# Two attention mixers' norms applied behind the projections, and a home of their own for the forget gates' weights

## What is computed

```python
    h = x
    for i in range(DEPTH):
        j = i // 2
        h = h + FFN_RES_SCALE * swiglu_2(rms_norm(h, ffa_norm[i]), ffa_w_gate_up[i], ffa_w_down[i])
        hn = rms_norm(h, mix_norm[i])
        if i % 2 == 0:
            h = h + even_mixer(hn, ev_w_in[j], ev_sinks[j], ev_cq_norm[j], ev_w_uq[j],
                               ev_ckv_norm[j], ev_w_ukv[j], ev_w_out[j])
        else:
            h = h + odd_mixer(hn, od_w_in[j], od_b_f[j], od_w_out[j])
        h = h + FFN_RES_SCALE * swiglu_2(rms_norm(h, ffb_norm[i]), ffb_w_gate_up[i], ffb_w_down[i])
        gate = jax.nn.sigmoid(rms_norm(h, ple_norm[i]) @ ple_w_gate[i])
        h = h + gate * (p[i] @ ple_w_proj[i])
    return rms_norm(h, final_norm)
```

## Time and profile before

| | |
|---|---|
| runs, median (lowest to highest) | 4158.46 us (4157.44 to 4158.93), 3 runs |
| profiled execution | 4156.04 us |
| its span | 4154.2 us |
| PE busy | 3963.3 us, 95% |
| DVE, ACT, POOL busy | 2038.6, 1314.0, 457.4 us |
| mean granted clock of TensorE | 0.974 |

### The profile page before, as it was taken

One profiled execution on the slowest core, in us unless ns is written; L12 is line 12 of the kernel. 1 busy time (PEld: TensorE's weight loads), 2 busy tenths in 40 slices (PEclk: granted clock), 3 DMA queues, 4 the chain that ended last, 5 costly groups with the idle time before them and its releaser, 6 DMA issues.

```text
span 4154.2 us, 47658 instructions
## 1 busy us (share of the span) xinstructions
PE 3963.3 (95%) x19618; PEld 3262.3 (79%) x19618; DVE 2038.6 (49%) x3065; ACT 1314.0 (32%) x1964; POOL 457.4 (11%) x509
## 2 busy tenths in 40 slices
PE   8988889999989999999999989999999999999997
PEld 5678889788867887888888766888778878778886
DVE  6545565646356765433443444433543343553445
ACT  3225344322232223222322345322332232342223
POOL 0015543100001111000200034000100000010001
PEclk9899999999999999999999999999999999999999
DMA  6220002445231112332322311232232223012322
GB/s 208 77 71 1 1 1 92 129 150 188 83 108 50 45 42 92 99 104 90 103 92 90 103 59 41 90 104 77 96 108 91 90 83 103 21 52 91 105 79 75
DMA packets 344098, 351.26 MB, mean 85 GB/s; under 512 B 9547, under 2 KB 340107, under 8 KB 343628
## 3 DMA queue, kind: packets, MB, share of 16 engines
q1 hardware_dynamic: 343884, 348.22, 26.2%
HBM read 345.83 MB, written 2.10 MB: 84 GB/s over the span
## 4 chain that ended last, share of the span: by engine, by line
PE 89%; DVE 5%; ACT 3%; issue 2%; DMA 1%; POOL 0%; POOLq 0%; SPq 0%; DVEq 0%; ACTq 0%
PE ps L371 23%; PE ps L372 23%; PE ps L373 23%; PE ps L1495 4%; PE ps L2417 3%; PE ps L2374 1%; PE ps L378 1%; ACT whi L347 1%; PE ps L3292 1%; PE ps L458 1%; PE ps L460 1%; PE ps L459 1%; DVE wlo L353 1%; PE ps L3279 1%; PE ps L764 1%
## 5 line engine op out<-in xcount | busy, mean ns | idle before, releaser
L353 DVE TENSOR_TENSOR wlo<-raw,whi 128x2048 fp32r<-128x2048 f32 (+6 forms) x315 | 627.7, 1993 | 988.7 <-ACT whi L347 988.7
L371 PE MATMUL ps<-Xh,whi 128*128 128x512 f32 x2640 | 1042.4, 395 | 23.8 <-DVE wlo L353 10.0
L372 PE MATMUL ps<-Xl,whi 128*128 128x512 f32 x2640 | 1034.6, 392 | 0.0
L373 PE MATMUL ps<-Xh,wlo 128*128 128x512 f32 x2640 | 1034.2, 392 | 0.0
L347 ACT ACTIVATE whi<-raw 128x2048 fp32r<-128x2048 f32 (+6 forms) x315 | 521.8, 1656 | 1127.2 <-PE ps L373 1114.2
L371 PEld LDWEIGHTS ps<-Xh,whi 128*128 128x128 f32 x2640 | 499.5, 189 | 137.0 <-issue 31.2
L372 PEld LDWEIGHTS ps<-Xl,whi 128*128 128x128 f32 x2640 | 499.5, 189 | 105.9 <-issue 2.0
L373 PEld LDWEIGHTS ps<-Xh,wlo 128*128 128x128 f32 x2640 | 499.0, 189 | 106.4 <-issue 0.5
L371 PE MATMUL ps<-HDh,whi 128*128 128x512 f32 x1056 | 411.7, 390 | 0.0
L373 PE MATMUL ps<-HDh,wlo 128*128 128x512 f32 x1056 | 410.9, 389 | 0.0
L372 PE MATMUL ps<-HDl,whi 128*128 128x512 f32 x1056 | 410.8, 389 | 0.0
(11 more groups left out here) (556 smaller groups left out, 5592.4 us busy)
## 6 DMA issues: line engine op xcount, KB each, us to landing
raw<-in_ffn_w SPq DMA_DIRECT2D x44, 1024.0 KB, 5.3
raw<-in_ffa_w_gate_up SPq DMA_DIRECT2D x44, 1024.0 KB, 5.0
raw<-in_ffb_w_gate_up SPq DMA_DIRECT2D x44, 1024.0 KB, 5.0
mslot<-in_mod_w SPq DMA_DIRECT2D x28, 1024.0 KB, 7.9
raw<-in_mod_w SPq DMA_DIRECT2D x20, 1024.0 KB, 6.0
raw<-in_ab_w_in SPq DMA_DIRECT2D x14, 1024.0 KB, 5.2
raw<-in_ffn_w SPq DMA_DIRECT2D x16, 768.0 KB, 4.4
raw<-in_hy_w_in SPq DMA_DIRECT2D x12, 1024.0 KB, 5.1
```

What stands on the lines that cost most here:

```text
L353: dve.tensor_tensor(k.part(k.wlo, c), k.raw(c), k.part(k.whi, c).bitcast(F32), ALU.subtract).then_inc(*k.ev.put("dve_wlo", ("lo", n), ("ra ...
L371: pe.matmul(o, wh, xh, start=first, stop=False)
L372: pe.matmul(o, wh, xl, start=False, stop=False)
L373: return pe.matmul(o, wl, xh, start=False, stop=last)
```

## The change

n6 and n10 become LATE. Their sum of squares keeps the compact form: one group of sum matmuls stands behind the first run of the mixer (`late_sum_pe`), the spread one block later (`spread_pe`), and ACT copies the spread 1/rms to SBUF (`late_rs_act`). Every projection's eviction then multiplies by it, by column for transposed results (rstd) and as ACT's scale for av and fv (rcol). For fq and fk, DVE multiplies in the PSUM bank itself ("scaled"), and ACT and DVE read the bank as before. krope's multiply is on POOL. In the even mixer the sums for cq and ckv move from behind krx to behind aq's second block. The forget gates' chunk is loaded and split during a1's down part 1 into a buffer of its own; fq's second chunk takes the slot that this frees. negc and c2 move two blocks back.

```diff
+        "n6": ("mix", 0), "n10": ("mix", 1)}
+EARLY = ("n1", "n2", "n3", "n13")
+COMPACT = EARLY + ("n6", "n10")
@@ weights_in_order
+                if (st, part, cc) == ("a1", 1, 2):
+                    W.add(("fl", 0), "od_w_in_2", (0,), 0, 8, 3072, 16, False)
-            W.add(("fq", 0), "od_w_in_2", (0,), 0, 8, 0, 256)
-            lin("fl", "od_w_in_2", 8, 3072, 16)
-            for cc in range(1, 12):
+            for cc in range(12):
@@ new
+def late_sum_pe(k, pe, tag):
+    ps = k.psum[NB]
+    pe.wait_ge(*k.ev.at(("sqsum", tag, 7)))
+    for t in range(4):
+        ins = pe.matmul(ps[:, t:t + 1], k.sq[2][:, t * 128:t * 128 + 128], k.onesD[:, 0:1], start=t == 0, stop=t == 3)
+    ins.then_inc(*k.ev.put("pe_sum", ("summed", tag, 7)))
+def late_rs_act(k, act, tag):
+    act.wait_ge(*k.ev.at(("rstd", tag)))
+    act.activation(k.rstd[:, :], k.bk.of(("rs", tag))[:, :], ACT.Copy).then_inc(
+        *k.ev.put("act_std", ("rs copy", tag), ("out", "rs", tag)))
@@ even_pe
     lin_pe(k, pe, "cq", keys_of("cq", 256), 8, k.X, lambda kk: [("x", "n6", kk)], together=2)
+    late_sum_pe(k, pe, "n6")
     lin_pe(k, pe, "ckv", keys_of("ckv", 128), 8, k.X, none)
+    spread_pe(k, pe, "n6")
     lin_pe(k, pe, "krx", keys_of("krx", 128), 8, k.X, none)
--    pe.wait_ge(*ev.at("o256"))
...
-    lin_pe(k, pe, "aq", keys_of("aq", 512), 8, k.X, none)
+    def after(m, ends):
+        if m == 1:
+            pe.wait_ge(*ev.at("o256"))
...
+    lin_pe(k, pe, "aq", keys_of("aq", 512), 8, k.X, none, after=after)
@@ even_dve
+    h_norm_dve(k, dve, "n6")
     next_lo(k, dve, ("ckv", 0))
+    dve.wait_ge(*ev.at(("rs copy", "n6")))
+    for st, m, dst in (("cq", 0, k.cq[:, 0, :]), ("cq", 1, k.cq[:, 1, :]), ("ckv", 0, k.ckv[:, 0, :])):
+        dve.wait_ge(*ev.at(("mm", st, m, 0)))
+        dve.tensor_tensor(dst, k.bk.of((st, m, 0))[:, :], k.rstd[:, :], ALU.mult).then_inc(
+            *ev.put("dve_even", ("out", st, m, 0)))
@@ odd_pe
     def after(m, ends):
+        if m == 1:
+            late_sum_pe(k, pe, "n10")
         if m == 2:
+            spread_pe(k, pe, "n10")
+        if m == 4:
              ps = room(k, pe, ("negc",))
             pe.wait_ge(*ev.at("lf"))
...
-        if m == 5:
+        if m == 7:
             turned_pe(k, pe, "c2", k.cd, ALL7)
@@ odd_act
+    root_table(k, act)
     next_hi(k, act, ("fq", 0))
+    h_norm_act(k, act, "n10")
+    late_rs_act(k, act, "n10")
 ...
-            if m % 2:
-                next_hi(k, act, (st, (m // 2) * 256) if (st, m) != ("fq", 1) else ("fl", 0))
-            act.wait_ge(*ev.at(("mm", st, m, 0)))
+            if m % 2 and (st, m) != ("fq", 1):
+                next_hi(k, act, (st, (m // 2) * 256))
+            act.wait_ge(*ev.at(("scaled", st, m)))
@@ odd_dve
+    h_norm_dve(k, dve, "n10")
+    dve.wait_ge(*ev.at(("rs copy", "n10")))
+    dve.tensor_tensor(r[:, 0, :], k.bk.of(("fl", 0, 0))[0:16, :], k.rstd[0:16, :], ALU.mult).then_inc(
 ...
+            dve.wait_ge(*ev.at(("mm", st, m, 0)))
+            ps = k.bk.of((st, m, 0))[:, :]
+            dve.tensor_tensor(ps, ps, k.rstd[:, :], ALU.mult).then_inc(*ev.put("dve_odd", ("scaled", st, m)))
+            if m % 2 and (st, m) != ("fq", 1):
+                next_lo(k, dve, (st, (m // 2) * 256))
             dve.wait_ge(*ev.at(("hi", st, m)))
```

More of the change, by code:

```diff
@@ L408, in lin_together_pe @@
             if kk == kt - 1:
-                ins.then_inc(*k.ev.put("pe_lin", ("mm", st, m, 0), *([("used", c.n)] if ends else [])))
+                ins.then_inc(*k.ev.put("pe_lin", ("mm", st, m, 0), *([("used", c.n)] if ends and c.n is not None else [])))
 def lin_pe(k, pe, st, keys, kt, X, xkeys, widths=((0, 512),), among=ALL7, after=None, together=0, lead=(), first=0):
@@ L2942, in even_act @@
     ev = k.ev
-    act.wait_ge(*ev.at(("mm", "cq", 0, 0)))
-    act.activation(k.cq[:, 0, :], k.bk.of(("cq", 0, 0))[:, :], ACT.Copy).then_inc(*ev.put("act_even", ("out", "cq", 0, 0)))
-    square_act(k, act, "cq", 0, k.cq[:, 0, :], made=("out", "cq", 0, 0))
+    root_table(k, act)
     next_hi(k, act, ("cq", 0))
[L2947 to L2950, removed]
+    h_norm_act(k, act, "n6")
     next_hi(k, act, ("ckv", 0))
+    late_rs_act(k, act, "n6")
+    for i in range(2):
+        square_act(k, act, "cq", i, k.cq[:, i, :], made=("out", "cq", i, 0))
+    act.wait_ge(*ev.at(("out", "ckv", 0, 0)))
+    act.activation(k.rq[1][:, :], k.ckv[:, 0, :], ACT.Square).then_inc(*ev.put("act_sq", ("sq", "ckv", 0)))
     next_hi(k, act, ("krx", 0))
@@ L3039, in even_dve @@
     dve.wait_ge(*ev.now())
-    dve.tensor_tensor(kr, kr, kt, ALU.add).then_inc(*ev.put("dve_mla", "krope"))
-    rstd_dve(k, dve, "cq", k.rq[0][:, :])
-    rstd_dve(k, dve, "ckv", k.rq[1][:, :])
-    apply_dve(k, dve, "cq", lambda i: k.cq[:, i, :], 2, L, k.rq[0][:, :], lambda i: k.col("cq", i), None, k.CQ)
+    dve.tensor_tensor(kr, kr, kt, ALU.add).then_inc(*ev.put("dve_mla", "krope sum"))
     for m in range(4):
@@ L3110, in even_pool @@
     pool.memset(k.kz[0:64, 1, 1, :], 0.0).then_inc(*ev.put("pool_mla", "kz zero"))
+    pool.wait_ge(*ev.at("krope sum"))
+    pool.tensor_tensor(k.krr[64:128, :], k.krr[64:128, :], k.rstd[64:128, :], ALU.mult).then_inc(
+        *ev.put("pool_mla", "krope"))
     pool.wait_ge(*ev.at(("mm", "av", 0, 3)))
@@ L3145, in odd_mem @@
     k.c2 = k.sb("c2", [128, L], R0 + 116 * K, F32R)
+    k.own = [k.sb("flw", [128, 8, 16], R0 + 86 * K + 512 * i, F32R) for i in range(2)]
     k.negc = k.sb("negc", [128, 4, 16], R0 + 124 * K)
@@ L3209, in filled_dve, with own_hi_act, own_lo_dve @@
     ins.then_inc(*k.ev.put("dve_fox", (name, "filled")))
+def own_hi_act(k, act):
+    c = k.W[("fl", 0)]
+    act.wait_ge(*k.ev.at(("raw", c.j)))
+    act.wait_ge(*k.ev.at(("hd", "a1", 1, 9)))
+    act.activation(k.own[0][:, :, :], k.raw3(c), ACT.Copy).then_inc(*k.ev.put("act_whi", "own hi"))
+def own_lo_dve(k, dve):
+    c = k.W[("fl", 0)]
+    dve.wait_ge(*k.ev.at("own hi"))
+    dve.tensor_tensor(k.own[1][:, :, :], k.raw3(c), k.own[0][:, :, :].bitcast(F32), ALU.subtract).then_inc(
+        *k.ev.put("dve_wlo", "own lo", ("raw free", c.j)))
 def odd_pe(k, pe):
@@ L3690, in pool_prog @@
     own_norm_pool(k, pool)
-    early_pool(k, pool, "n6")
+    gained_pool(k, pool, "n6")
     even_pool(k, pool)
```

77 lines of the change are left out of this document (45 added, 32 removed).

## The result

The changed kernel takes 4129.13 us (median of 4 runs, 4126.78 to 4131.73) against 4158.69 us for the kernel before in the same measurement: ratio 0.9924, 95% interval 0.9911 to 0.9936, so 29.6 us less. Two later measurements gave 29.0 and 29.1 us less. Forecast were 24.6 us less, at 4133.9 us with a range from 4130.3.

A forecast was written before the change was run, and what follows sets the result against it. PE, busy 95% of the span, was taken as the bound; 12.2 us off the first mixer and 12.4 off the second, 24.6 together, gave 4131.4, plus 2.4 to the runs' median 4133.9 us, range 4130.3 to 4139.6.

The forecast's parts named there:

- Removed: PE's stalls, waits and the slow clock behind them at both mixers go: 14.9 us in the first, 16.4 us in the second.
- One compact sum of 4 fp32 matmuls (1.05 us), one spread (1.26 us) and about 0.4 us of changeovers: Work added bare on PE in each mixer, 2.7 us each; before, it lay inside the stall.
- rival with cheaper changeovers: Second mixer has no new wait, DVE through 1.3 us sooner, and 0.8 us of changeovers vanish: 4131.8 us, chance 0.10.
- First mixer 14.9 - 2.7 = 12.2 us. Second 16.4 - 2.7 - 1.3 = 12.4 us. Together 24.6 us off: Sum over both mixers: time removed less work added on PE and the second's 1.3 us wait, 24.6 us gained.
- The 2.4 us between the profiled run and the median: Whole kernel: the runs' median lies 2.4 us above the profiled execution, so 4131.4 us becomes 4133.9 us.
- The new wait: Second mixer at fq 6: PE waits 1.3 us for fq 768's low half, range 1.0 to 3.4 us, without slow clock.
- The links: Each fq block, second mixer: multiply in PSUM, hi on ACT, lo on DVE, 0.73 + 0.63 + 0.61 = 1.97 us.
- rival with a longer backlog: Second mixer: forget-gate chain 2 us later, PE waits 3.3 us and pays 2.2 us slow clock: 4138.1 us, chance 0.17.
- Parts at nothing in the mixers and the FFNs in front: Extra copies, multiplies, splits and loads on ACT, DVE, POOL and SP in mixers and FFN down parts cost PE zero.
- a lost cover: First mixer: the norms' stall covered late weights or splits, so PE waits 2.3 us plus 1.7 us slow clock: 4137.9, chance 0.10.
- longer down parts: Both FFNs' down parts: gained tiles lengthen DVE's queue, each of 16 half chunks makes PE wait 2.1 us: 4166.8, chance 0.02.
- The home's 6.8 us: Second mixer: forget gates' weights in their own buffer remove a 4.6 us wait for fq 256 and 2.2 us slow clock.

The follow-up runs named there:

- sums_four: The changed kernel with the sum and the spread of both mixers issued four times each, 16 matmuls instead of 4: 4147.06 us, ratio 0.9962 to the kernel before.
- delay3: The changed kernel with three more 128x512 multiplies on DVE before fq 0's eviction: 4134.28 us, ratio 0.9931 to the kernel before.
- ring: The changed kernel with the forget gates' weights left in the two weight slots, both norms late: 4153.51 us, ratio 0.9984 to the kernel before.
- even_only: The kernel before with only the first mixer's functions of the changed kernel, its norm late: 4144.56 us, ratio 0.9967 to the kernel before.
- split_ahead: The changed kernel with fq 768's split behind fq's first eviction instead of the third's: 4129.86 us, ratio 0.9925 to the kernel before; repeated, 4132.92 us, 0.9930.

## Why the prediction missed by 5 us

**Removed: right.** What each mixer lost, worked back from the stages with the price of sum and spread as measured: first 13.33 + 1.8 added = 15.1 us (forecast 14.9), second 13.40 + 1.8 + 1.2 for the new wait = 16.4 us (forecast 16.4). The granted clock of 1.00 at both mixers and the missing gaps are the evidence.

**"One compact sum of 4 fp32 matmuls (1.05 us), one spread (1.26 us) and about 0.4 us of changeovers": too dear.** This step failed in size. I read the busy time of a group and added changeovers to it. But that time runs past the start of the next matmul (0.95 us for the sum in the changed kernel, the next start after 0.81), and the 1.26 us of the spread stood partly at the lower clock, where the changed kernel has 1.05. What PE loses is the time to the next matmul's start, 0.81 us, and 0.09 us in that matmul (0.32 us to the next one, not 0.23). Measured four times over it is 0.89 us. That makes 1.8 us a mixer for 2.7, which is 1.8 us of the miss in both; rounding and the terms above give the other 0.3 us in the mixers. Half of the rival with cheaper changeovers was right; its other half, no wait, was not.

**"First mixer 14.9 - 2.7 = 12.2 us. Second 16.4 - 2.7 - 1.3 = 12.4 us. Together 24.6 us off": the sum took every other stretch as unchanged.** The second failed step, and the larger: it is worth 3.6 us, put at nothing without a reason. Between the mixers a wait for weights in the ple stage fell from 2.04 to 1.77 us and the slow clock behind it went. The row and the window of the stretch from it on, before and changed:

```profile
2991.99 0.47 PE L371 MATMUL ps<-X2h,whi 128*128 128x512 f32 x1 [2.04 <-DVE wlo L353]
2982.23 0.47 PE L377 MATMUL ps<-X2h,whi 128*128 128x512 f32 x1 [1.77 <-DVE wlo L359]
```
```profile
2991.90:3009.20 17.30, 15.47 (x60) 0.90 0.24 76
2982.20:2997.80 15.60, 13.88 (x60) 1.00 0.25 85
```

The stretch is 961.7 to 961.9 us in all four kernels with the first norm early, 959.8 to 960.0 in all with it late but for sums_four (957.95). Behind the second mixer the forget-attention stage takes 94.0 us three times in the changed kernel and 95.6 in before. Why the wait got shorter and why the clock differs in the same instructions is not settled; that it goes with the arrangement of the code and is not chance is shown by the repeats. 24.6 + 2.1 + 3.6 = 30.3 us, against 29.0 to 29.6 measured. The 2.4 us between the profiled run and the median were rightly added: that run had a short start.

**The new wait: right.** Forecast for fq 6 at 41.2 us from the switch (the first matmul on X, 3375.50), low half ready at 42.5, 1.3 us, clock unchanged. Measured: due at 40.9 (3416.38 - 3375.50), ready at 42.0, wait 1.07, next matmul 0.47, clock 1.00. The links hold: rstd used from 24.7 (25.0), first eviction at 32.6 (33.2), the multiply in PSUM takes 0.69 us, as taken. The rival with a longer backlog priced 2 us late at 4.2; delay3 shows 1.8 in the mixer, because the lateness is split over a bank and a low half (1.11 and 1.67 us), and the clock stays at 1.00 behind either.

**Parts at nothing in the mixers and the FFNs in front: right.** PE waits nowhere in the first mixer's projections, and both FFNs in front switch without a gap. The rivals of a lost cover and of longer down parts have nothing in the trace.

**The home's 6.8 us: right in size, but not a term by itself.** With the norm as before it is 7.1 us in the stage, and only where negc stands later and the split is behind the apply. Alone the home costs 3.8 us, and without it, as in ring, the change keeps only 8 of its 29 us. I priced it by the wait that it removes, and overlooked that this wait covered the forget-gate chain. The move of negc (and c2), which I counted as no term, turns 4.2 us more in the stage into 4.1 less, and the place of the split gives the other 3.0.

## What to carry to other kernels

Price a group put bare into a dense stream of matmuls by start to next start, not by its busy time, which here ran 0.14 to 0.24 us past the next start. Before an edit that removes a wait is priced alone, list what reached its due time only because of that wait: here the home without the late norm made the second mixer 4.2 us longer, the late norm without the home 10.6 us longer, and both with the later negc 13.4 us shorter. And where the granted clock changes, measure stages, not only the total: a gain of 1.3 us in one stage was given back whole in the next.

## What the runs showed of the hardware

The granted clock is not decided by the length of the last wait alone. The same 1.88 us wait for a low half, with 0.40 us matmuls behind it in the changed kernel (first row), has 0.63 us matmuls behind it in even_only (second row and window):

```profile
3013.60 0.47 PE L377 MATMUL ps<-Xh,whi 128*128 128x512 f32 x1 [1.88 <-DVE wlo L359]
3018.41 0.67 PE L373 MATMUL ps<-Xh,whi 128*128 128x512 f32 x1 [1.88 <-DVE wlo L355]
```
```profile
3018.40:3024.00 5.60, 5.59 (x18) 0.70 0.55 187
```

It also fell without any wait, in sixteen 128x1 matmuls in a row (0.68 from inside the group in sums_four's first mixer) or right behind them (in its second). Behind the start, what the slow clock costs in one kernel repeats: three executions of the changed kernel and two of split_ahead agree stage by stage to 0.2 us, though the two of split_ahead start 5.7 us apart. So there it goes with the kernel and not with the time at which a stage runs. The start itself does not repeat; it took 2350.0 to 2351.0 us in the changed kernel and 2348.6 and 2354.3 in split_ahead. Equal instructions of the forget-attention stage took 94.0, 95.3, 95.6, 98.5 and 101.5 us in five arrangements; what in the arrangement decides that was not found.
